# Centering and scaling of the gated recurrence: done inside the sample attention or at the recurrence's start

## The reference

```python
f = lb + (1.0 - lb) * sigmoid(hf)
q, k, i, logf = silu(hq), 1.0 - f, hi, log(f)
# per chunk: b = cumsum(logf); S is the state
inter = (q * exp(b)) @ S
decay = exp(where(causal, b[t] - b[s], -inf))      # per feature
A = sum_k q[t] * decay[t, s] * k[s]
o = inter + A @ i
S_new = exp(b_last) * S + (k * exp(b_last - b)).T @ i
```

## Time and profile before

| | us |
|---|---|
| median of 3 timed runs (lowest to highest) | 3493.36 (3487.78 to 3494.72) |
| the profiled execution | 3487.69 |
| its span, first to last instruction | 3485.9 |
| PE busy in it | 3237.3 (93%) |
| DVE busy | 2573.2 (74%) |
| ACT busy | 1313.3 (38%) |
| POOL busy | 1024.4 (29%) |
| mean granted clock of PE | 0.956 |

### The profile page before, as it was taken

One profiled execution on the slowest core, in us unless ns is written; L12 is line 12 of the kernel. 1 busy time (PEld: TensorE's weight loads), 2 busy tenths in 40 slices (PEclk: granted clock), 3 DMA queues, 4 the chain that ended last, 5 costly groups with the idle time before them and its releaser, 6 DMA issues. The chain is left out here.

```text
span 3485.9 us, 54537 instructions
## 1 busy us (share of the span) xinstructions
PE 3237.3 (93%) x20435; PEld 1974.0 (57%) x20435; DVE 2573.2 (74%) x5334; ACT 1313.3 (38%) x2581; POOL 1024.4 (29%) x1074
## 2 busy tenths in 40 slices
PE   7999986898999887999999999996999999999997
PEld 4668652664466544656565565653555555555554
DVE  4222653444432699999999999986888888888887
ACT  3000552321200224677676677652222222222222
POOL 0000000000000003988999899862111111111110
PEclk9999998777999999999999999998999999999998
DMA  3220887324222353878888777889887877877873
GB/s 146 96 96 31 289 301 308 135 97 159 98 77 77 134 192 138 255 266 292 282 282 283 266 279 270 284 320 385 304 294 283 305 295 281 304 294 283 302 287 150
DMA packets 213104, 803.41 MB, mean 230 GB/s; under 512 B 33824, under 2 KB 92320, under 8 KB 169088
## 3 DMA queue, kind: packets, MB, share of 16 engines
q1 hardware_dynamic: 176000, 531.81, 41.9%
q0 software_dynamic: 36864, 268.45, 21.9%
HBM read 665.19 MB, written 201.98 MB: 249 GB/s over the span
## 5 line engine op out<-in xcount | busy, mean ns | idle before, releaser
L1682 PE MATMUL psum<-arena 128*128 128x400 f16 x6144 | 1099.4, 337 | 47.4 <-DVE arena L1730 46.9
L2039 PE MATMUL psum<-arena 128*128 128x400 f16 x6144 | 1049.4, 332 | 24.3 <-DVE arena L2085 24.3
L1682 PEld LDWEIGHTS psum<-arena 128*128 128x128 f16 x6144 | 598.2, 99 | 477.1 <-DVE arena L1730 55.7
L2039 PEld LDWEIGHTS psum<-arena 128*128 128x128 f16 x6144 | 596.5, 97 | 477.1 <-DVE arena L2085 24.7
L1654 POOL TENSOR_SCALAR arena<-arena 128x128 f16<-128x128 f16 x800 | 712.2, 903 | 54.9 <-DVEq L1860 26.4
L116 POOL DMA_INDIRECT arena<-in_experts,arena x256 | 300.3, 1173 | 1178.1 <-DVE arena L149 1081.6
L135 ACT ACTIVATE arena<-arena 128x1 f32<-128x1 f32 x256 | 51.6, 202 | 915.3 <-DVE arena L128 915.1
L149 DVE SCALAR_TENSOR_TENSOR arena<-arena 128x1024 f32<-128x1024 f32 x256 | 330.4, 1291 | 17.6 <-issue 3.2
L2092 DVE TENSOR_TENSOR arena<-arena,psum 128x800 f32<-128x800 f32 x256 | 251.9, 984 | 108.0 <-PE psum L2039 108.0
L128 DVE CUSTOM_DVE_ANT_0 arena<-arena 128x1024 f32<-128x1024 f32 x256 | 311.3, 1218 | 18.9 <-DMA arena<-in_experts,arena 17.9
L1911 ACT ACTIVATE arena<-arena 128x128 f16<-128x128 f16 x800 | 245.1, 388 | 85.6 <-DVE arena L1868 85.5
(11 more groups left out here) (230 smaller groups left out, 3505.5 us busy)
## 6 DMA issues: line engine op xcount, KB each, us to landing
arena<-in_u_feat SPq DMA_DIRECT2D x128, 512.0 KB, 6.9
arena<-in_experts SPq DMA_DIRECT2D x128, 512.0 KB, 5.3
scratch_acts<-arena SPq DMA_DIRECT2D x128, 400.0 KB, 5.0
arena<-scratch_gates SPq DMA_DIRECT2D x32, 1600.0 KB, 8.0
arena<-scratch_acts SPq DMA_DIRECT2D x128, 400.0 KB, 6.5
scratch_gates<-arena SPq DMA_DIRECT2D x48, 1024.0 KB, 6.7
out_k_win_sample<-in_cache_k SPq DMA_DIRECT2D x32, 1022.0 KB, 21.1
out_v_win_sample<-in_cache_v SPq DMA_DIRECT2D x32, 1022.0 KB, 21.6
```

What stands on the lines that cost most here:

```text
L1682: last = pe.matmul(psum[:, 2 * p + k, 0:SLD], w[:, s, q, :], xs[:, q, k * SLD:(k + 1) * SLD], start=q == 0 and w is u_hi and xs is x_hi, s ...
L2039: last = pe.matmul(psum[:, 2 * (n % BANKS) + i, 0:SLD], w[:, s, k, q * P:(q + 1) * P], hs[:, s, k, i * SLD:(i + 1) * SLD], start=k == 0 an ...
```

## The change

The centering, the two exponentials and the scaling of keys and queries leave hgrn and are done in attend_sample. b is centered in place in `f`, with the middles of the chunks copied aside first (`middle`, `middle_s`). `carry` and `carry_s` get a place at the end of the arena that both blocks leave alone. exp(-f) is made head by head in `falling`, which is the buffer of `resets`; the heads alternate between ACT and DVE. copy_turned(1) stands between the second and third head on ACT, and write_out(0) between the second and third scaling on DVE. In hgrn PE and SP no longer wait for DVE at the start (`keys_scaled` and `step_dve` go); DVE zeroes `sum_state` before its wait for the loads. The load of bias_sample goes behind the keys of sequences 0 and 1.

```diff
@@ -46,6 +46,7 @@
...
 BIAS0 = WORDS - SEQ
+CARRY0 = WORDS - 4 * (NCH + 1) - 2 * 4 * SB
 
...
@@ -183,6 +184,8 @@
...
             "row_slots": at(SLOT0, SLOTS, 2 * D), "row_sums": at(SUM0, 2, D), "x_row": at(XROW0, D),
+            "carry": at(CARRY0, G, NCH + 1),
+            "carry_s": at(CARRY0 + G * (NCH + 1), 2, G * SB).rearrange("p a (g b) -> p a g b", g=G),
             "row_index": at(IDX0, 2, P).bitcast(U32), "row_weight": at(WGT0, 2, P),
...
@@ -587,13 +590,12 @@
...
         k = mix[:, 4:8, :]
-        ek = at(word, G, T); word += GT
+        word += SB * 512
         causal = at(word, P); word += P
...
         hnorm = at(word, 1); word += 1
-        carry = at(word, G, NCH + 1); word += G * (NCH + 1)
-        carry_s = at(word, 2, G * SB).rearrange("p a (g b) -> p a g b", g=G); word += 2 * G * SB
+        carry, carry_s = m["carry"], m["carry_s"]
         state = at(word, 4, G, P); word += 4 * G * P
...
@@ -601,16 +603,14 @@
...
         inv = at(word, G * P); word += G * P
-        assert word <= WORDS, word
+        assert word <= CARRY0, word
         eq = at(F0, G, T)
...
         loaded = sem("hgrn_loaded")
-        step_act = sem("hgrn_act")
         step_dve = sem("hgrn_dve")
-        keys_scaled = sem("hgrn_keys_scaled")
         turn_ready = sem("hgrn_turn_ready")
...
@@ -651,7 +651,6 @@
...
                 shift_window(sp, x, n, windows_shifted)
-            sp.wait_ge(step_dve, 1)
             sp.dma_start(w_half, x["w_out"][:, 0:4, :]).then_inc(w_half_loaded, 16)
...
@@ -671,13 +670,6 @@
...
         def _(act):
-            act.wait_ge(step_dve, 1)
-            act.activation(ek, eq, ACT.Exp, scale=-1.0).then_inc(step_act, 1)
-            act.drain()
-            act.activation(eq, eq, ACT.Exp)
-            act.activation(carry[:, :, 1:], carry[:, :, 1:], ACT.Exp)
-            act.activation(carry_s, carry_s, ACT.Exp).then_inc(step_act, 1)
-
             for t in range(9):
...
@@ -696,6 +688,7 @@
...
 
+            act.wait_ge(step_dve, 1)
             for n in range(NCH):
...
@@ -718,7 +711,6 @@
...
         def _(pe):
-            pe.wait_ge(keys_scaled, 1)
             for t in range(9):
...
@@ -728,7 +720,6 @@
...
             pe.wait_ge(turn_copied, 9)
-            pe.wait_ge(step_dve, 2)
 
...
@@ -809,7 +800,7 @@
...
                           masked[0:NS, g, 0:NS], start=g == 0, stop=False, skip_group_check=True)
-            pe.wait_ge(step_dve, 3)
+            pe.wait_ge(step_dve, 2)
             for g in range(G):
...
@@ -832,34 +823,9 @@
...
         def _(dve):
+            dve.memset(sum_state[:, 0], 0.0)
+            dve.drain().then_inc(step_dve, 1)
             dve.wait_ge(loaded, 16 * 5)
-            mid, mid_s = CH // 2 - 1, ST // 2 - 1
-            chunks = b[:, :, 0:SEQ].rearrange("p g (n c) -> p g n c", c=CH)
-            chunks_s = b[:, :, SEQ:T].rearrange("p g (n c) -> p g n c", c=ST)
-            for g in range(G):
-                dve.tensor_tensor(eq[:, g, 0:SEQ].rearrange("p (n c) -> p n c", c=CH), chunks[:, g],
-                                  chunks[:, g, :, mid:mid + 1].broadcast_to([P, NCH, CH]), ALU.subtract)
-                dve.tensor_tensor(eq[:, g, SEQ:T].rearrange("p (n c) -> p n c", c=ST), chunks_s[:, g],
-                                  chunks_s[:, g, :, mid_s:mid_s + 1].broadcast_to([P, SB, ST]), ALU.subtract)
-            dve.drain()
-
-            ends = eq[:, :, 0:SEQ].rearrange("p g (n c) -> p g n c", c=CH)[:, :, :, CH - 1]
-            ends_s = eq[:, :, SEQ:T].rearrange("p g (n c) -> p g n c", c=ST)[:, :, :, ST - 1]
-            dve.tensor_copy(carry[:, :, NCH], ends[:, :, NCH - 1])
-            dve.memset(carry[:, :, 0], 1.0)
-            dve.tensor_tensor(carry[:, :, 1:NCH], ends[:, :, 0:NCH - 1], chunks[:, :, 1:NCH, mid], ALU.add)
-            dve.tensor_copy(carry_s[:, 0], chunks_s[:, :, :, mid_s])
-            dve.tensor_copy(carry_s[:, 1], ends_s)
-            dve.drain()
-            dve.tensor_scalar(eq, eq, 40.0, -40.0, ALU.min, ALU.max)
-            dve.drain().then_inc(step_dve, 1)
-            dve.wait_ge(step_act, 1)
-            dve.memset(sum_state[:, 0], 0.0)
-            dve.tensor_tensor(k, k, ek, ALU.mult)
-            dve.drain().then_inc(keys_scaled, 1)
-            dve.wait_ge(step_act, 2)
-            dve.tensor_tensor(q, q, eq, ALU.mult)
-            dve.drain().then_inc(step_dve, 1)
 
...
@@ -970,7 +936,7 @@
...
         SLOT = 4 * NKEY
-        assert KT * 512 == SLOT and word + 2 * SLOT <= WORDS
+        assert KT * 512 == SLOT and word + 2 * SLOT <= CARRY0
         slot_words = (word, word + SLOT, F0, F0 + SLOT)
...
@@ -981,9 +947,15 @@
...
         lbt = at(word, 8, G); word += 8 * G
+        q, carry, carry_s, falling = feat[:, FHQ, :, :], m["carry"], m["carry_s"], resets
+        middle = at(word, G, NCH); word += G * NCH
+        middle_s = at(word, G, SB); word += G * SB
         assert word <= F0 + 8 * T
...
         decay_dve = sem("decay_dve")
+        falling_ready = sem("falling_ready")
+        keys_scaled = sem("keys_scaled")
+        rising_ready = sem("rising_ready")
         constants_loaded = sem("sample_constants_loaded")
...
@@ -1003,8 +975,6 @@
...
         def _(sp):
-            sp.dma_start(bias, x["bias_sample"]).then_inc(constants_loaded, 16)
-
             def load_keys(b):
...
@@ -1019,6 +989,7 @@
...
             load_keys(1)
+            sp.dma_start(bias, x["bias_sample"]).then_inc(constants_loaded, 16)
             sp.wait_ge(new_ready, 9)
...
@@ -1133,6 +1104,33 @@
...
 
+            def center_decays():
+                mid, mid_s = CH // 2 - 1, ST // 2 - 1
+                chunks = f[:, :, 0:SEQ].rearrange("p g (n c) -> p g n c", c=CH)
+                chunks_s = f[:, :, SEQ:T].rearrange("p g (n c) -> p g n c", c=ST)
+                dve.tensor_copy(middle, chunks[:, :, :, mid])
+                dve.tensor_copy(middle_s, chunks_s[:, :, :, mid_s])
+                dve.drain()
+                for g in range(G):
+                    dve.tensor_tensor(chunks[:, g], chunks[:, g],
+                                      middle[:, g].unsqueeze(2).broadcast_to([P, NCH, CH]), ALU.subtract)
+                    dve.tensor_tensor(chunks_s[:, g], chunks_s[:, g],
+                                      middle_s[:, g].unsqueeze(2).broadcast_to([P, SB, ST]), ALU.subtract)
+                dve.drain()
+                ends, ends_s = chunks[:, :, :, CH - 1], chunks_s[:, :, :, ST - 1]
+                dve.tensor_copy(carry[:, :, NCH], ends[:, :, NCH - 1])
+                dve.memset(carry[:, :, 0], 1.0)
+                dve.tensor_tensor(carry[:, :, 1:NCH], ends[:, :, 0:NCH - 1], middle[:, :, 1:NCH], ALU.add)
+                dve.tensor_copy(carry_s[:, 0], middle_s)
+                dve.tensor_copy(carry_s[:, 1], ends_s)
+                dve.drain()
+                dve.tensor_scalar(f, f, 40.0, -40.0, ALU.min, ALU.max)
+                dve.drain().then_inc(decay_dve, 1)
+
+            def scale_keys(g):
+                dve.wait_ge(falling_ready, g + 1)
+                dve.tensor_tensor(k[:, g, :], k[:, g, :], falling, ALU.mult).then_inc(keys_scaled, 1)
+
             def add_bias(r):
...
@@ -1166,9 +1164,17 @@
...
             normalize(1)
+            center_decays()
+            scale_keys(0)
+            scale_keys(1)
             write_out(0)
+            scale_keys(2)
+            scale_keys(3)
+            dve.wait_ge(rising_ready, 1)
+            dve.tensor_tensor(q, q, f, ALU.mult).then_inc(keys_scaled, 1)
             write_out(1)
             dve.wait_ge(out_done, 2 * H)
+            dve.wait_ge(keys_scaled, G + 1)
 
...
@@ -1196,8 +1202,18 @@
...
                 act.activation(silu, silu, ACT.Silu)
-            copy_turned(1)
+            act.wait_ge(decay_dve, 3)
+            for g in range(G):
+                if g >= 1:
+                    act.wait_ge(keys_scaled, g)
+                act.activation(falling, f[:, g, :], ACT.Exp, scale=-1.0).then_inc(falling_ready, 1)
+                if g == 1:
+                    copy_turned(1)
             act.drain()
+            act.activation(f, f, ACT.Exp)
+            act.activation(carry[:, :, 1:], carry[:, :, 1:], ACT.Exp)
+            act.activation(carry_s, carry_s, ACT.Exp)
+            act.drain().then_inc(rising_ready, 1)
 
...
```

## The result

| | us |
|---|---|
| before, median of 20 runs | 3492.10 (3486.15 to 3499.04) |
| after, median of 20 runs | 3484.86 (3478.48 to 3489.62) |
| ratio, 95% interval | 0.9979 (0.9972 to 0.9985) |
| profiled execution of after, its span | 3487.19, 3485.4 |

The change takes 7.24 us off, 0.21%; 7.4 were forecast. The profiled executions of the two kernels happen to lie only 0.5 us apart (3487.69 and 3487.19), so the gain has to be read from the stages, not from the two spans.

A forecast was written before the change was run, and what follows sets the result against it. Body bound by TensorE and its clock; in the head TensorE idled behind a serial chain. 0.6 (bias) + 9.0 (head) - 2.2 (half clock) = 7.4 us less, from 3490.6: 3483 us, range 3478 to 3489 (8 in 10: 3474 to 3492).

The forecast's parts named there:

- The moved part is free: Sample attention: centering and scalings fit VectorE's gaps before its two write_outs, 2.6 and 3.6 us of cover left, costing nothing.
- The transposes: Head of the recurrence: TensorE's transposes move from 619.83 to about 593.1, 26.7 us earlier.
- The wait that takes the place: First half projection: TensorE waits 17.7 us for output weights queued behind seven shifts; 9.0 of 26.7 us are kept.
- first rival: Head: output weights slip past the shifts, up to 26.7 + 0.6 us gained, no 2.2 us lost: 3463; chance 0.07.
- Ring order: DMA queue: descriptors are consumed in the order put there, so earlier issue behind the same shifts buys nothing; 9.0 us.
- The restart at half clock: First half projection: after the wait TensorE runs 4.3 to 5.4 us at half clock, 2.2 us lost (2.2 to 2.7).
- The bias: Start of sample attention: bias load behind the first keys gains 0.6 us, between 0 and 2.2.
- The body's clock: Body of the recurrence: low-clock stretches at later tiles last 6.75 or 13.5 us, as they happen to fall.
- the step of 3.4 us: Later tiles: each 6.75 us step of low clock is worth 3.4 us, for or against.
- the middle of four times: Level of before: 3490.6 us, from the profiled execution and three timed runs, instead of the profiled 3487.69.
- The rival of a slower result: Body: low-clock stretches at six tile boundaries all take 13.5 us, 10 us more: 3493; chance 0.09.
- VectorE being late: Sample attention: VectorE late for write_out, work beyond 2.6 us of cover delays it; 5 us over gives 3485.6; chance 0.06.

The follow-up runs named there:

- the changed kernel's second profile: The kernel after, unedited, run again on another chip as the level for runs beside it: 3485.46 us, ratio 0.9977 to the kernel before.
- Experiment 5: Changed kernel with the clip of the centered decays repeated: once more (2.4 us of VectorE) 3485.99 us; three times more (7.3 us) 3492.82 us.
- experiment 1: Changed kernel with the half output weights' load issued right behind the state's load, ahead of x rows and seven window shifts: 3465.2 us, ratio 0.9921.
- experiment 2: Changed kernel with the load of the half output weights issued after three of the seven window shifts: 3476.39 us, ratio 0.9948 to the kernel before.
- Experiment 4: Changed kernel with the bias_sample load back in front of the keys of sequences 0 and 1: 3483.85 us, ratio 0.9971 to the kernel before.
- experiment 3: The filler: changed kernel with 16 TensorE products before its wait for the output weights: 3483.0 us; again, beside the changed kernel, 3480.31 us.

## Why the prediction was right

The forecast was 3483 us, the time is 3484.86; 7.4 us less, and it is 7.24. That the two agree to 0.2 us is in part luck: the interval of the ratio leaves 5 to 10 us, and attention, head and restart as measured add up to 5.4 us less in the profile of after (0.45 + 9.12 - 4.14) and to 6.5 in the changed kernel's second one (-0.22 + 8.61 - 1.92), the clock of the rest of the body left aside. By its steps, in the profile of after:

- **The moved part is free.** Centering was to end at 561.8 and ended at 561.69 (559.33 + 2.36). The two scalings were to end at 566.5 with 2.6 us of cover, and ended at 566.90 with 2.80. The query scaling was to end at 585.9 with 3.6 us, and ended at 585.28 with 3.70. The two copies that no row had sized took 0.28 and 0.19 us. Experiment 5 shows that the cover is no larger than it looks: 2.4 us more leave no gap.
- **The transposes** start at 592.56 (593.1 was said), the first masked product at 604.57 (605.1), behind the state's arrival as forecast: what ended VectorE's wait is TensorE, not the DMA.
- **The wait that takes the place.** Reached at 616.35 (633.94 - 17.59; 616.8 was said), ended at 633.94 (634.5), 17.59 us long (17.7). The change keeps 9.12 us in the head: it was 643.55 - 593.00 = 50.55 and is 633.94 - 592.51 = 41.43 us (41.8 to 42.4 in four other traces with the same head, hence 8.2 to 9.1 us). Experiments 1 and 2 show that the place in the queue is the whole cause of the wait: the landing moves with the shifts ahead of it, and without them the 17.6 us and the restart are gone. This was the first rival's mechanism, "the weights come early", which the change by itself does not bring and which one moved line does. It was priced at 3463; the kernel that has it takes 3465.2. Ring order, which the Trainium skill states (DMA: Bandwidth & Descriptors, "Queues, rings and completion order"), agrees with these traces: 26.4, 16.7 and 12.3 us to landing by place in the queue.
- **The restart at half clock** was the weakest term. I took 4.3 to 5.4 us at half speed from two rows, 2.2 us lost. In the profile of after the clock is low until 642.25, 8.3 us, and from the first to the third half projection it takes 9.36 us where before took 5.22: 4.1 us lost. But in the changed kernel's second profile the same stretch takes 7.14 us (633.32 to 640.46), 1.9 lost, and in experiments 4 and 5, which leave this part alone, 6.73, 6.86 and 7.33. So in four of five executions 1.5 to 2.1 us are lost, a little under the term, and in the fifth its upper bound of 2.7 us was too low.
- **The bias** was worth 0.6 us by the sum. The attention as a whole is 0.45 us shorter in this pair of profiles; the earlier start of the scores (1.8 us) is mostly lost again, as forecast. The clock took part too: in before it slowed the first of two products with values (7.90 us, then 6.20), in after the second (6.20, then 7.51). Experiment 4 doesn't resolve a term of this size.
- **The body's clock** is why the two profiled spans lie so close. Of the 7.4 us that the body of after is longer in this pair (215.19 against 207.76), 4.1 are the restart; the other 3.3 are where the clock happened to fall in the tiles. From the third half projection on, the body takes 202.5 us in before and 202.6 in the first filler trace, but 205.8 in after, 205.6 in its second profile and 205.6 in experiment 1, which has no restart at all; TensorE is busy 183.7 us of it in the first two, at a granted clock of 0.79, and 186.8 in the others, at 0.77 to 0.78, while VectorE's busy time is the same. That is about the step of 3.4 us that I had reckoned. So part of the 207.83 us in experiment 3 is luck too, and as before was profiled once only, no run shows which length is usual for it. To forecast from the middle of four times rather than from the profiled one was right: it was the fastest of them, and the median of 20 runs of before is 3492.10.

The rival of a slower result had the clock falling badly in every tile; the median of 20 runs doesn't show that. VectorE being late did not happen; its price can be read from experiment 5. With 7.3 us over, the rule of that rival gives 7.3 - 2.6 = 4.7 us lost, and the attention lost 3.2. The medians lose the whole gain there, but in the profiled pair two thirds of the difference lie outside the attention, where no instruction was added, so they don't tell the price of the cover.

## What to carry to other kernels

When a chain is moved off the critical path, ask what each later instruction will wait for next, and look for transfers that were hidden only by the chain: here 17.6 of 27 us went to a load whose issue had become free, but not its place in the queue. Moving the change's own dependence one step further, the now early load ahead of copies that nobody waits for, was worth almost three times the change itself. Cover is to be read at each point where the engine is next needed (2.8 and 3.7 us here), not from the engine's idle share.

## What the runs showed of the hardware

- DRAM to DRAM copies of 1022 KB ahead of it on the same queue hold a load of 2048 KB back: it took 26.4 to 27.6 us to land behind seven, 16.7 behind three, that is some 2.4 us more from issue to landing for each, and 3.0 us with the later issue. With only the state's load ahead of it (2048 KB too) it took 12.3.
- In the two profiles of the changed kernel, after waiting for 17.59 and 18.66 us, TensorE's first products of 128x512 ran at half clock (1.2 GHz: 3.78 us for four instead of 1.96 at 2.4 GHz), for 3.7 us in the second (633.32 to about 637.0) and for 8.3 in the first (633.94 to 642.25). Here the granted clock of the 0.25 us in which it rose again (PEclk is the third number from the end):

```profile
642.25:642.50 0.25, 0.25 (x2) 0.01 (x1) 0.00 (x0) 0.00 (x0) 0.00 (x0) 0.86 0.00 0
```

- After an idle time of 2.63 us the same products ran at the full clock. After one of 4.75 us they started at it, but the granted clock fell to half at about 634.1 (0.75 from 634.00 to 634.25, 0.50 behind it), 0.5 us after the first of them began. After one of 5.50 us (experiment 2) the first four took 3.71 us.
- Two profiled executions of kernels that are the same in the blocks behind the recurrence differed by up to 9.3 us there (2632.0 to 2641.3).
